# Layers of a two-block transformer kernel without a barrier between them, squares and result in parts

## The reference

```
for l in range(2):                       # first block
    h = rmsnorm(x, g_mix_pre[l])
    mix = concat(gated_deltanet(h), dsa_attention(h), hgrn2(h)) @ w_out[l]
    x = x + rmsnorm(mix, g_mix_post[l])
    h = rmsnorm(x, g_ffn_pre[l])
    x = x + rmsnorm((gelu(conv(h @ up)_gate) * conv(h @ up)_val) @ down, g_ffn_post[l])
for l in range(2):                       # second block, mod = silu(c) @ w_ada[l] + b_ada[l]
    x = x + 0.5 * gate(0) * swiglu(norm_mod(x, 0), up[l, 0], down[l, 0])
    x = x + gate(1) * mixer(norm_mod(x, 1))
    x = x + 0.5 * gate(2) * swiglu(norm_mod(x, 2), up[l, 1], down[l, 1])
```

## Time and profile before

| | us |
|---|---|
| median of 3 runs | 4203.4 (4200.63 to 4210.62) |
| the profiled execution | 4203.58 |
| its span | 4202.0 |
| TensorE matmul busy | 3850.1 (92%) |
| VectorE busy | 2188.6 (52%) |
| ScalarE busy | 1163.6 (28%) |
| GpSimd busy | 306.3 (7%) |
| mean granted TensorE clock | 0.959 |

### The profile page before, as it was taken

How to read it: one execution, slowest core, us unless ns; L and a number is a source line. 1 busy time by engine, 2 the same in 40 slices (tenths; PEclk the granted TensorE clock), 3 DMA queues, 4 the chain that set the end, 5 groups by cost and what they waited for, 6 DMA issues and landing times.

```text
span 4202.0 us, 51863 instructions
## 1 busy us (share of the span) xinstructions
PE 3850.1 (92%) x18598; PEld 3041.9 (72%) x18598; DVE 2188.6 (52%) x3548; ACT 1163.6 (28%) x1714; POOL 306.3 (7%) x503
## 2 busy tenths in 40 slices
PE   6998889896999788898899999899989999999998
PEld 4778657785788747777688786488868887756886
DVE  3767547754667636763554455355433335444332
ACT  2331323222332313221222233222222223332221
POOL 1110001110020001110111010011100001000000
PEclk9998899998999889999999999999999999999999
DMA  3310024441320014443455330155423333103332
GB/s 84 81 35 1 10 76 142 141 129 52 91 65 1 1 50 125 140 136 96 119 159 148 97 84 11 51 155 160 131 75 95 90 96 84 45 17 84 100 87 84
DMA packets 579512, 359.93 MB, mean 86 GB/s; under 512 B 20366, under 2 KB 559744, under 8 KB 579328
## 3 DMA queue, kind: packets, MB, share of 16 engines
q1 hardware_dynamic: 553920, 281.43, 24.3%
q0 software_dynamic: 25408, 76.11, 6.0%
HBM read 355.35 MB, written 2.10 MB: 85 GB/s over the span
## 4 chain that ended last, share of the span: by engine, by line
PE 74%; DVE 12%; DMA 5%; issue 4%; ACT 2%; DVEq 1%; POOLq 1%; SPq 0%; POOL 0%; ACTq 0%
PE ps L1231 13%; PE ps L1232 13%; PE ps L1233 13%; PE ps L1463 6%; PE ps L1467 6%; PE ps L1466 6%; PE ps L1284 5%; DMA wada<-in_w_ada 5%; PE ps L1585 3%; DVE wl L1951 2%; PE ps L1387 2%; DVE ada_sum L2096 1%; PE ps L1345 1%; PE ps L1367 1%; PE ps L1747 1%
## 5 line engine op out<-in xcount | busy, mean ns | idle before, releaser
L1231 PE MATMUL ps<-hh,wh 128*128 128x512 f32 x2816 | 1123.4, 399 | 91.5 <-DVE wl L1951 64.2
L1232 PE MATMUL ps<-hl,wh 128*128 128x512 f32 x2816 | 1104.7, 392 | 0.0
L1233 PE MATMUL ps<-hh,wl 128*128 128x512 f32 x2816 | 1104.6, 392 | 0.0
L1951 DVE TENSOR_TENSOR wl<-wring,wh 128x1024 fp32r<-128x1024 f32 x476 | 581.4, 1223 | 800.5 <-ACT wh L752 785.7
L752 ACT ACTIVATE wh<-wring 128x1024 fp32r<-128x1024 f32 x496 | 522.7, 1055 | 1033.8 <-PE ps L1463 507.5
L1231 PEld LDWEIGHTS ps<-hh,wh 128*128 128x128 f32 x2816 | 534.0, 190 | 237.1 <-issue 104.8
L1233 PEld LDWEIGHTS ps<-hh,wl 128*128 128x128 f32 x2816 | 533.5, 189 | 113.4
L1232 PEld LDWEIGHTS ps<-hl,wh 128*128 128x128 f32 x2816 | 534.6, 190 | 108.3 <-issue 1.9
L1463 PE MATMUL ps<-ah,wh 128*128 128x512 f32 x1056 | 411.7, 390 | 1.9 <-DVE wl L1951 1.9
L1467 PE MATMUL ps<-ah,wl 128*128 128x512 f32 x1056 | 410.9, 389 | 0.0
L1466 PE MATMUL ps<-al,wh 128*128 128x512 f32 x1056 | 410.8, 389 | 0.0
(11 more groups left out here) (394 smaller groups left out, 4054.0 us busy)
## 6 DMA issues: line engine op xcount, KB each, us to landing
wring<-in_w_ffn_up SPq DMA_DIRECT2D x176, 512.0 KB, 4.9
wada<-in_w_ada POOLq DMA_DIRECT2D x384, 192.0 KB, 2.8
wring<-in_w_in SPq DMA_DIRECT2D x98, 512.0 KB, 5.0
wring<-in_ffn_w_up SPq DMA_DIRECT2D x88, 512.0 KB, 4.9
wring<-in_w_ffn_down SPq DMA_DIRECT2D x64, 512.0 KB, 3.6
wring<-in_w_out SPq DMA_DIRECT2D x32, 512.0 KB, 4.9
wring<-in_ffn_w_down SPq DMA_DIRECT2D x32, 512.0 KB, 3.6
wring<-in_w_ffn_down SPq DMA_DIRECT2D x16, 384.0 KB, 3.4
```

Source lines behind the costliest of these rows:

```text
L1231: pe.matmul(dst, w, h, start=first, stop=False)
L1232: pe.matmul(dst, w, hlo, start=False, stop=False)
L1233: return pe.matmul(dst, wlo, h, start=False, stop=last)
L1951: v.tensor_tensor(wl[:, w, :, :], wring[:, p, h, :, :], wh[:, w, :, :].bitcast(F32), ALU.subtract)\
```

## The change

1. The layers of the first block are written out on every engine. `turn`, `end`, `layer_end` and `layer_go` go. Shared semaphores are never cleared and count on from layer to layer; those used only in the mixers (`in_mixers`) are cleared by POOL during the following down projection, after its own loads, and engines wait for `mixers_clear` at the start of the next layer.
2. `post_norm` adds each x tile right after it is scaled, with one tile of delay. The last `post_norm` of a first-block layer takes the next layer's first two splits into `wide_root`. The next layer's squares are made per x tile. In the second block the second layer's first norm is summed in the down projection before.
3. In `pairs` of a `conv_first` part the second split stands before the taps of the second tile.
4. The result: 16 transposes are made inside the last down projection after `DOWN_END[5]`, 12 more at its last tile but one, 4 at the end; DVE copies six pieces, ACT two; SP stores it with three DMAs, the first (1 MB) in the down projection.

```diff
-        layer_end = ev("layer_end")
-        layer_go = ev("layer_go")
-        tick = ev("tick")
+        mixers_left = ev("mixers_left")
+        mixers_clear = ev("mixers_clear")
+        out_act = ev("out_act")
...
+        result = hT[:, :, :].rearrange("p k t -> p (k t)").rearrange("p (n d) -> p n d", n=NT)
+        out_rows = out.rearrange("b (n p) d -> p (b n) d", p=P)
+        HALF = D // 2
...
-            with sp.Fori(0, DEPTH) as l:
+            for l in range(DEPTH):
...
-            sp.wait_ge(out_cp.sem, 2 * NT)
-            sp.dma_start(out.rearrange("b (n p) d -> p (b n) d", p=P),
-                         arena[:, 0:NT * D].rearrange("p (n d) -> p n d", n=NT)).then_inc(out_done.sem, 16)
-            sp.wait_ge(out_done.sem, 16)
+            sp.wait_ge(out_cp.sem, NT)
+            sp.dma_start(out_rows[:, :, 0:HALF], result[:, :, 0:HALF]).then_inc(out_done.sem, 16)
+            sp.wait_ge(out_cp.sem, NT + 2)
+            sp.dma_start(out_rows[:, 0:2, HALF:D], result[:, 0:2, HALF:D]).then_inc(out_done.sem, 16)
+            sp.wait_ge(out_act.sem, 2)
+            sp.dma_start(out_rows[:, 2:4, HALF:D], result[:, 2:4, HALF:D]).then_inc(out_done.sem, 16)
+            sp.wait_ge(out_done.sem, 48)
...
-            def turn(n):
-
-                g.wait_ge(layer_end.sem, n)
-                g.sem_inc(tick.sem, 1)
-                g.wait_ge(tick.sem, 1)
-                for s in scoped:
-                    g.sem_clear(s.sem)
-                g.sem_inc(layer_go.sem, 1)
+            def clear_mixers(layer):
+
+                g.wait_ge(mixers_left.sem, 3 * (layer + 1))
+                for x in in_mixers:
+                    g.sem_clear(x.sem)
+                g.sem_inc(mixers_clear.sem, 1)
...
-            turn(3)
-            with g.Fori(0, DEPTH) as l:
+            for l in range(DEPTH):
                 for n in range(POOL_SPLITS):
                     p, h = (11 + n // 2) % 2, n % 2
-                    g.wait_ge(w_hi.sem, 21 + n)
+                    g.wait_ge(w_hi.sem, l * TILES_1 + 21 + n)
...
-                conditioning(ada[0], l * (ADA // 2), 0)
-                turn(l * 3 + 6)
+                conditioning(ada[0], l * (ADA // 2))
+                clear_mixers(l)
...
@@ scalar @@
-            end(1)
-
-            with s.Fori(0, DEPTH) as l:
+            s.preload_act_table_set("sqrt_and_others")
+
+            for l in range(DEPTH):
                 begin(l * (SLOTS_1 // 2))
-                s.preload_act_table_set("sqrt_and_others")
+                enter(l)
                 split()
                 split()
+                wide_norm([xT[:, k, :] for k in range(KD)], lambda k: (x_ready if l else xt_copied).next(s))
                 par_ready.next(s)
-                wide_norm([xT[:, k, :] for k in range(KD)])
                 parts()
...
                 begin(l * (SLOTS_2 // 2) + DEPTH * SLOTS_1 // 2)
+                enter(DEPTH + l)
                 split()
+                if l:
+                    wide_norm([])
                 split()
+                if not l:
+                    wide_norm([xT[:, k, :] for k in range(KD)], lambda k: x_ready.next(s))
                 par_ready.next(s)
-                wide_norm([xT[:, k, :] for k in range(KD)])
...
+                ffn(ACT.Silu, False, second_square if l + 1 < DEPTH else None)
+
+            for n in (2, 3):
+                s.wait_ge(out_tr.sem, NT + n + 1)
+                s.activation(result[:, n, HALF:D], ps[:, 4 + n, :], ACT.Copy).then_inc(out_act.sem, 1)
...
@@ tensor @@
+            def out_part(ks):
+
+                for n in range(NT):
+                    for k in ks:
+                        m = pe.transpose(ps[:, 4 + n, k % 4 * P:(k % 4 + 1) * P], xT[:, k, n * P:(n + 1) * P], ident[:])
+                    if ks[-1] % 4 == 3:
+                        m.then_inc(out_tr.sem, 1)
...
+                    if last and n == DOWN_END[5]:
+                        pe.wait_ge(x_ready.sem, X_UPDATES - KD + 4)
+                        out_part(range(4))
+                    if last and n == NF - 2:
+                        pe.wait_ge(x_ready.sem, X_UPDATES - 1)
+                        pe.wait_ge(out_cp.sem, NT)
+                        out_part(range(4, 7))
...
@@ vector @@
-                for k in range(KD):
-                    v.scalar_tensor_tensor(hT[:, k, :], hT[:, k, :], g(k), ps[:, 6, :], ALU.mult, ALU.mult)
-                v.drain()
-                for k in range(KD):
-                    v.tensor_tensor(xT[:, k, :], xT[:, k, :], hT[:, k, :], ALU.add).then_inc(x_ready.sem, 1)
+                for k in range(KD + 1):
+                    if k < KD:
+                        v.scalar_tensor_tensor(hT[:, k, :], hT[:, k, :], g(k), ps[:, 6, :], ALU.mult, ALU.mult)\
+                            .then_inc(dve_order.sem, 1)
+                    if k:
+                        dve_order.next(v)
+                        v.tensor_tensor(xT[:, k - 1, :], xT[:, k - 1, :], hT[:, k - 1, :], ALU.add)\
+                            .then_inc(x_ready.sem, 1)
                 v.drain()
...
                             beside()
+                            split(whole=last and j == 1)
                             later(i, j, 1)
-                            split(whole=last and j == 1)
                             beside()
...
+                        if last and DOWN_END.index(n) == 5:
+                            for m in range(NT):
+                                v.wait_ge(out_tr.sem, m + 1)
+                                v.tensor_copy(result[:, m, 0:HALF], ps[:, 4 + m, :]).then_inc(out_cp.sem, 1)
...
-                post_norm(lambda k: par[:, 0, A_G + 24 + k:A_G + 25 + k])
-                end(l + 2)
+                post_norm(lambda k: par[:, 0, A_G + 24 + k:A_G + 25 + k], 2)
...
-                split()
-                split()
-                mod_norm(0)
-                n_sq[0] += KD
+                if l:
+                    split()
+                mod_norm(0, 1 if l else 0)
+                if not l:
+                    n_sq[0] += KD
```

More of the change, by code:

```diff
@@ L717, in _ @@
                 if l + 1 < DEPTH:
[L718 to L719 removed]
+                    conditioning(ada[l + 1], ADA // 2)
+                    clear_mixers(DEPTH + l)
         @block.scalar
@@ L765, in parts, with leave_mixers, enter @@
                             .then_inc(h_hi.sem, 1)
-            def end(go):
-                s.drain().then_inc(layer_end.sem, 1)
-                s.wait_ge(layer_go.sem, go)
+            def leave_mixers():
+                s.drain().then_inc(mixers_left.sem, 1)
+            def enter(layer):
+                if layer:
+                    s.wait_ge(mixers_clear.sem, layer)
             def square(src):
@@ L1201, in _, with begin, all_free, enter @@
             n_norm = [0]
-            def begin(turns):
-                for x in scoped:
+            def begin(turns, first_bank):
+                for x in in_mixers:
                     x.restart(id(pe))
                 place[:] = [turns, 0]
-                n_split[0] = n_mm[0] = n_sq[0] = n_norm[0] = 0
-                pe.sem_inc(mm_done.sem, 1)
-            def end(go):
-                pe.drain().then_inc(layer_end.sem, 1)
-                pe.wait_ge(layer_go.sem, go)
+                n_split[0] = 0
+                n_mm[0] = first_bank
+            def all_free():
+                at = mm_free.seen.setdefault(id(pe), [0, 0])
+                pe.wait_ge(mm_free.sem, at[0] + at[1] + 4)
+            def enter(layer):
+                if layer:
+                    pe.wait_ge(mixers_clear.sem, layer)
             def loaded(i=None):
@@ L1494, in _ @@
                 m.then_inc(xt_done.sem, 1)
-            end(1)
-            with pe.Fori(0, DEPTH) as l:
-                begin(l * (SLOTS_1 // 2))
-                n_mm[0] = 2
+            pe.drain().then_inc(mm_done.sem, 1)
+            pe.wait_ge(const_ready.sem, 2)
+            for l in range(DEPTH):
+                begin(l * (SLOTS_1 // 2), 2)
+                enter(l)
+                all_free()
                 wide_norm()
@@ L1907, in _ @@
                 summed_norm()
-                ffn(ada=l + 1 < DEPTH, squares=False)
-                end(l + 4)
-            for n in range(2 * NT):
-                if n >= 4:
-                    pe.wait_ge(out_cp.sem, n - 3)
-                for k in range(4):
-                    m = pe.transpose(ps[:, n % 4, k * P:(k + 1) * P],
-                                     xT[:, 4 * (n % 2) + k, (n // 2) * P:(n // 2 + 1) * P], ident[:])
-                m.then_inc(out_tr.sem, 1)
+                pe.drain().then_inc(mixers_left.sem, 1)
+                ffn(ada=l + 1 < DEPTH, squares=l + 1 < DEPTH, last=l + 1 == DEPTH)
+            pe.wait_ge(x_ready.sem, X_UPDATES)
+            out_part(range(7, 8))
         @block.vector
@@ L1923, in _, with begin, enter, leave_mixers @@
             link = Order(v, dve_order)
-            def begin(loads):
-                for x in scoped:
+            mm_done.seen[id(v)] = [0, 1]
```

(26 more changed lines are left out.)

82 lines of the change are left out of this document (44 added, 38 removed).

## The result

The kernel after takes 4051.7 us (median of 4 runs, 4049.9 to 4055.9) against 4205.2 for the kernel before (4 runs): a ratio of 0.9636, 95% interval 0.9619 to 0.9653. Five further runs of the same kernel, beside nine others of the kernel before, gave 4056.1 (4048.4 to 4061.1) and a ratio of 0.9655 (0.9632 to 0.9678).

A forecast was written before the change was run, and what follows sets the result against it. TensorE, busy 92% of the span, was taken as the bound, so only its standstills or work count. Gains 10.8 + 22.2 + 17.4 + 16.3 + 6.6 + 49 + 11.8 = 134.1 from 4203.6 gave 4069; range 4056 to 4121.

The forecast's parts named there:

- The start: Kernel start: ACT no longer waits for POOL's clears, so the whole start moves earlier by 10.8 us.
- the two joins behind the first block's layers: Ends of layers 1 and 2: no barrier, squares made per added tile; gains of 22.2 and 17.4 us.
- the join to the fourth layer: Third to fourth layer: squares summed already in the down projection, first scaled tile sooner; gain 16.3 us.
- the norm behind the mixers: Two norms after the first block's mixers: TensorE's sums end sooner after the additions, 3.3 us each, 6.6 together.
- the end: Kernel end: most transposes inside the last down projection, result stored in pieces; gain 11.8 us, between 9.7 and 13.6.
- part 2: End of layer 1: first scaled tile of the next norm at 1015.9 instead of 1038.09; gain 22.2 us.
- part 6: First block's up projections: split before the taps requests weights earlier, so DVE's `wada` piece is not late; gain 49 us.
- Rival A: Up-projection loop keeps its 12.7 us per j, by collision as before or the page's rule; 4115 us, chance 0.24.
- Rival B: At four joins, issue waits or the weights' first slot take the barrier's place; + 14, 4083 us, chance 0.09.
- C: First block's 42 trips: earlier weights delay both c's and d's pieces, up to 2.3 us per trip; 4215, chance 0.02.
- D: A layer might still wait for `mixers_clear`, needing clears 100 us later than the rows allow; chance 0.01.
- bound of 54: Upper bound of the up-projection loop's gain, if the wait before the loop and the restart cost both go.

The follow-up runs named there:

- the second execution: The profiled execution of the kernel after, repeated unchanged beside the kernel before: span 4059.0 us; median of those runs 4056.1, ratio 0.9655.
- run 1: Kernel after with only the second split of the first block's up projection put back behind the taps: 4109.0 us, ratio 0.9780.
- run 2: Kernel after, split still ahead of the taps, but the ring slot it frees given back only behind them: 4104.1 us, ratio 0.9766.
- run 3: Kernel before with only the up projection's second split moved ahead of the taps: 4140.3 us, ratio 0.9845.
- run 10: Kernel after with the second split one place further ahead, before DVE's step c: 4078.3 us, ratio 0.9718.
- the bare kernel: Kernel after with the barrier back behind the first and second layers, without the 118 clears, splits behind it again: 4070.6 us, ratio 0.9692.

## Why the prediction was right, and where it was wrong

**Right, part by part.** The start (10.8 against 10.7), the two joins behind the first block's layers (22.2 and 17.4 against 22.0 and 17.5), the join to the fourth layer (16.3 against 15.7), the norm behind the mixers (3.3 against 3.2) and the end (11.8 against 12.4) came out as worked out. So did what was to be seen: no clear on the chain, TensorE's waits for the split below 10 us, a j of 11.3 us (11.5 in the second execution). At the end the 28 transposes cost 1.75 + 1.31 = 3.1 us, with a granted clock of 1.00, where the sum had 3.2, or 3.5 with two changes of work. (The prediction's last paragraph says that the last landing comes 10 us after the last update; its own sum has 6.3, and 6.7 to the span's end. Measured were 6.3 us from the last update's end at 4042.4 to the span's end at 4048.7.) In part 2 the 1.28 us of ACT's table load are inside the gain without having been named; the sum is right all the same, since it was built forward from the additions.

**The mechanism of part 6** is shown by runs 1, 2, 3 and 10: the order of the split and the taps sets when 1 MB of weights goes ahead of a piece of 192 KB. Rival A fell, both by the time and by run 2. Rival B fell too: the three joins came out within 0.6 us of a forecast without any new wait. C fell by the time, and D by the chain (POOLq 0%). One step of the mechanism was too hopeful: d's piece lands after 3.6 us and not "3", and DVE still waits 5.7 us in 14 steps. TensorE has slack for it.

**The step that failed: "The gain is what TensorE waits there, less the wait of 2.9 us that stands before the loop: 2 x 24.4 = 49".** The term was mis-sized: 49 in the sum, 56 to 61 measured. An idle counter begins where the last matmul is shown to end, and that is 0.392 - 0.227 = 0.165 us after the next one could have started. With 18 waits, 3.0 us of lost time counted as busy: 24.4 + 3.0 = 27.4. The trace's own starts say the same: over the 18 waits, the distances from one start to the next are 27.3 us longer than the usual 0.2275 us each. The Trainium skill, Perfetto Trace Analysis, "Summary: the profiler window per engine type", says that TensorE's end in a profile is an estimate; the row of L1258 agrees. Another 2.6 us lie in distances that are wider although no idle time is shown between the two matmuls. The split moved alone (run 3) brought 27.2 us in the first layer: 25.9 of waits and 1.3 of these. In the second it brought 29.7; there the loop of before also had 3.2 us of matmuls at the lower clock level and the same loop of run 3 had none (granted clock 0.99 from 1589.3 to 1858.3, 1.00 from 1562.0 to 1801.6). Whether the split has a part in that is not shown. The prediction's bound of 54, "if wait and restart cost both go", named such a cost but made it too small and left it out of the sum. I had the means to see it: the same 1068 matmuls stood twice in the trace of before, in the first block's up projection and in the second block's. Here they are: the stretch, its length, PE's busy time, and so on as above.

```profile
606.56:873.40 266.84, 242.45 (x1068) 195.81 (x1069) 192.76 (x272) 80.75 (x104) 47.12 (x84) 0.99 0.49 141
2034.90:2270.40 235.50, 235.50 (x1068) 196.04 (x1069) 134.13 (x190) 53.68 (x62) 45.69 (x85) 1.00 0.56 160
```

266.8 - 235.5 = 31.3 us was the most that the first layer's stretch could give: 27.3 of waits, 2.6 of wider distances and 1.6 in nine matmuls at the lower clock level, against 0.2 of all these in the second block's stretch. The gains were 26.8 to 29.2 us in the first layer and 29.3 to 32.0 in the second.

**The range** failed for this and for a second reason. Its low end of 4056 stood 13 us under the forecast, and nothing in the prediction sets it by how much one execution differs from the next, although the runs of before show it (4200.6 to 4210.6). The profiled execution of the kernel after lies 19 us below the sum: 12.4 by part 6 and 7.0 by the short mixers of the second layer, where the forecast had 3.3 us and no term for the clock. The second profiled execution, at 4060.7, lies 8 us below the forecast, 7.3 of it by part 6, and inside the range; the median of its five runs, 4056.1, is at the edge. So the mis-sized term alone would not have taken the time out of the range; the four runs of the result were also on the short side, and that was luck.

**Open.** What decides in an execution whether TensorE's clock falls for 65 us or for 78 to 89 in the mixers was not settled. Nor was why an up projection with the moved split takes anything from 255 to 262 us; DVE's waits for `wada` vary with it (5.7 us in 14 steps in one execution, 9.5 in 17 in the other), and the longest, 262.0 us in the bare kernel, had the lowest granted clock (0.976, the others 0.987 to 0.993). An experiment with four `wada` buffers, which might take that wait away, was not tried.

## What to carry to other kernels

Price a stall by the distance between the starts of the same work with and without it, not by the idle counter. Where an engine waits for a small transfer in every trip of a loop, look at which large transfer was released just before its issue: moving the release by one or two operations can be worth more than a barrier, and both directions must be tried, since one place too early only moves the collision. The end of a layer can hold four costs that are best counted one by one: the clears, the work that can't begin before the barrier, the loop's jump, and a table load at the loop's head. Look each piece of the chain up in the engine's timeline before naming it: what the chain calls issue can be an instruction.

## What the runs showed of the hardware

The landing time of a 192 KB load depends on its distance to the megabyte in front of it (two transfers of 512 KB): 2.6 us where the second of these was issued 5 us earlier or more, 3.6 where the first was issued 2.9 us earlier, 5.0 to 5.4 directly behind them. POOL's issue took 0.54 us in each case.

The same mixers, with the same matmuls, take 522 to 524 or 527 to 531 us, with 65 or with 78 to 89 us of it at TensorE's lower clock level. A kernel with such a stretch can't be compared by one profile to better than 7 us. Its other stretches can: down projection and join of the unchanged kernel repeated to 0.5 us (142.2 and 142.7, 141.9 and 141.9).

ACT's jump back to the head of a loop that holds a whole layer took 3.40 us, and a load of its table 1.28; 118 semaphore clears by POOL took about 8 us of the time of engines that wait for them.
